# Summing the fetched rows of two of four token tiles in PSUM, in a two-layer decoder kernel

## The chip, the cores and the metric

The kernel runs on one NeuronCore of a Trainium2 chip. The metric is the device time of one execution in microseconds (us); below 0.2% of it, some 3.4 us, a difference cannot be told from none. Engines are named as in the profile: PE is TensorE (PEld its weight loads), ACT is ScalarE, DVE is VectorE, POOL is GpSimd, SP is SyncE with its DMA queue (SPq).

## What is computed

Two layers on 512 tokens of 1024 float32 channels. Layer 0 mixes with a Mamba-2 and sparse-attention pair, layer 1 with a three-branch attention; each layer ends in a hierarchical mixture of experts, and that end is what matters here. Every token goes to two of 32 experts:

```python
for i in range(DEPTH):
    h = rms_norm(x, attn_norm[i])
    x = x + (even_mixer if i % 2 == 0 else odd_mixer)(h, ...)
    h = rms_norm(x, ffn_norm[i])
    x = x + hier_moe(h, ...)

# hier_moe, per token: the weighted sum of its two experts' rows
    def expert_block(args):
        xblk, e = args
        hid = jax.nn.silu(xblk @ w_gate[e]) * (xblk @ w_up[e])
        return hid @ w_down[e]
    yb = lax.map(expert_block, (xb, blk_expert)).reshape(n_rows, dm)
    y = jnp.zeros_like(xt).at[row_token].add(yb * row_weight[:, None].astype(yb.dtype))
```

## The kernel before

Tokens lie in four tiles of 128 (`NT` = 4); the residual `xt` holds them in SBUF, tile `i` as `xt[:, i, :]`. All queues are written by hand in program order, one instruction stream per engine, with semaphores between them.

**Experts.** `per_expert` runs 32 experts over a ring of three weight buffers: the first three, a loop, then experts 30 and 31 by hand (`after` = 1 and 0). For each expert PE multiplies gate and up in two halves (L1807), turns the hidden rows (L1813) and multiplies down (L1820); ACT copies the result out (L1902); POOL scatters 64 x 2 half-rows to `y_d` in DRAM. The last expert's rows are not scattered: behind expert 30, PE turns a matrix of weighted ones (L2078), ACT copies it to `last_T` (L2137), and after expert 31 eight matmuls (L2107) spread its 64 rows over all tokens, two per tile, into banks 2i and 2i+1.

**The end of a layer.** SP fetches the scattered rows back, one DMA per tile with both rows of each token (L2001, semaphores `m_yin0` to `m_yin3`). DVE then adds them tile by tile: `add_fetched(i)` is two instructions over 1024 channels (L2316), `add_last(i)` two over 512 that add PE's banks (L2323) and raise `m_x`. The order is fetched 0, fetched 1, last 0, fetched 2, last 1, fetched 3, last 2, last 3.

**What follows.** In layer 0, `odd_act` takes each tile's squares as it is ready (`norm_square`, L271), POOL makes the reciprocal root (`norm_pool`, L279 and L281), ACT the diagonal (`norm_diag`, L302), PE turns and scales the tile with it (`turn_pe`, L318, 16 recorded instructions a tile), DVE and ACT copy out (L332, L330), and the projection starts when all four are out (L1440). Three matmuls without use (L1431) stand ahead of the turning. In layer 1, SP writes each tile to the output (L2341). A float32 matmul is recorded as two PE instructions. In `moe_pool`, POOL waits at the end of a layer for all four counts of `m_fin`, the semaphore of L2107's tiles, before it goes on to `norm_pool`.

Of the kernel before, what the change touches and what calls it, by code (L numbers as in the profile page):

```python
# [22 lines left out]
P = 128  # L23
# [93 lines left out]
class Chain:  # L117
# [42 lines left out]
    "zeros": ("pads", 1), "y_zero": ("acol_in", 32), "m_fin": ("yd_mm", 4), "m_lturn": ("st_mm", 3), "m_lT": ("sq", 5),  # L160
    "m_lones": ("y_gated", 4), "mx0_yin": ("brow", 2), "mx1_yin": ("relb_ones", 1),
# [37 lines left out]
def build(nc, ins, out):  # L199
    ctx = ExitStack()  # L200
    with ctx:
# [66 lines left out]

        def norm_square(act, i):

            nc.scalar.activation(rows[:, i, :], xt[:, i, :], ACT.Square, scale=DM ** -0.5,  # L271
                                 accum_out=ss[:, i:i + 1]).then_inc(S("norm_sq"), 1)

        def norm_pool(pool, tag):
            for i in range(NT):
                n = NT * WHOLE[tag] + i + 1
# [20 lines left out]
        def norm_diag(act, tag, i):  # L297

            act.wait_ge(S("norm_rstd"), NT * 2 * WHOLE[tag] + i + 1)
            if i >= 2:  # L300
                act.wait_ge(S("turned"), 2 * NT * WHOLE[tag] + 2 * (i - 1))
            nc.scalar.activation(diag[:, i % 2], ident[:], ACT.Copy, scale=rstd[:, i:i + 1]).then_inc(S("diag"), 1)  # L302
# [8 lines left out]
        def turn_pe(pe, tag):  # L311

            for i in range(NT):
                pe.wait_ge(S("diag"), NT * WHOLE[tag] + i + 1)
                for half in range(2):
                    for k in range(4):
                        c = (4 * half + k) * P
                        mm = nc.tensor.matmul(bank[2 * i + half][:, k * P:(k + 1) * P], xt[:, i, c:c + P], diag[:, i % 2],  # L318
                                              start=True, stop=True)
                    mm.then_inc(S("turned"), 1)  # L320

        def turn_evac(eng, tag, i, half, on_act=False):

            eng.wait_ge(S("turned"), 2 * NT * WHOLE[tag] + 2 * i + half + 1)
            d = hT[:, 4 * half:4 * half + 4, i * P:(i + 1) * P]
            b = split(bank[2 * i + half][:, :], 4, P)
# [1071 lines left out]
        def odd_sp(sp):  # L1398
            sp.wait_ge(S("m_x"), 2 * NT)
# [320 lines left out]
        last_n = at(O_LAST + 4 * NT * CAP + NT * P, 3, 2 * NT)  # L1720
        wgu = [at(u * EW, 2, KD, FF) for u in range(RING)]
# [303 lines left out]
        def moe_pe(pe, L):  # L2025
# [33 lines left out]

            def body(e, c, cu, u, after):  # L2060
                gate_up(pe, t, c, cu, u)
# [39 lines left out]
            further(pe, t, L, more, last=lambda n: wait_apart(pe, (S(f"{x}_step"), n * X_STEPS + 1)))  # L2101
            pe.wait_ge(S("m_lT"), past("m_lT") + L + 1)
            pe.wait_ge(S(f"{t}_y"), L * NE + NE + 1)
            for i in range(NT):
                for h in range(2):
                    cs = slice(h * CAP, (h + 1) * CAP)
                    mm = nc.tensor.matmul(bank[2 * i + h][:, :], last_T[cs, i * P:(i + 1) * P], yb[cs, (NE - 1) % RING, :],  # L2107
                                          start=True, stop=True)
                mm.then_inc(S("m_fin"), 1)

        def moe_act(act, L):
# [12 lines left out]
            def body(e, c, cu, u, after):  # L2124
# [25 lines left out]
            further(act, t, L, more)  # L2150

# [21 lines left out]
        def moe_dve(dve, L, link):  # L2173
# [95 lines left out]
            def last_ones(c):  # L2269
# [13 lines left out]
                link(v_.tensor_tensor(flat(other_w[:]), keep, flat(weight[:]), ALU.mult))  # L2283
# [35 lines left out]
            def add_last(i):  # L2319
                dve.wait_ge(S("m_fin"), past("m_fin") + NT * L + i + 1)  # L2320
# [75 lines left out]
```

## Time and profile before

| | us |
|---|---|
| median of 3 runs | 1678.95 (1678.14 to 1682.0) |
| the profiled execution | 1680.21 |
| its span, first to last instruction | 1678.3 |

Mean granted clock of TensorE in the profiled execution: 0.984. Profile rows below give a start, a duration, the engine and line, the operation with what it writes and reads, a count, and in brackets how long the engine stood idle before it and what ended that. Merged rows (x16) run from the first start to the last end.

### The profile page before, as it was taken

What the parts mean: (1) busy time and instruction counts of PE and PEld (TensorE: products, weight loads), DVE (VectorE), ACT (ScalarE), POOL (GpSimd) and SP (SyncE); (2) the same over time, 40 slices, a digit from 0 to 9 for tenths busy, and PEclk for the clock granted to TensorE, in tenths of its full rate; (3) what the DMA queues carried; (4) which work ended last, traced back from release to release, by engine and by line L of the source; (5) the groups of instructions that cost most, each with busy time, mean ns of one, the idle gap of its engine ahead of it and who ended that gap; (6) DMA issues with size and microseconds to landing.
All of it is one profiled execution on the core that took longest, in us unless ns stands there. A gap on an engine that the chain in (4) does not pass through costs nothing.

```text
span 1678.3 us, 21100 instructions
## 1 busy us (share of the span) xinstructions
PE 1592.5 (95%) x7988; PEld 754.8 (45%) x7988; DVE 449.7 (27%) x1146; ACT 395.2 (24%) x899; POOL 199.4 (12%) x296
## 2 busy tenths in 40 slices
PE   7999899799999999999899989999799999999995
PEld 4545574433333333333446447865333333333332
DVE  1585751520000000001412235653500000000004
ACT  2444451211111111111200236642211111111110
POOL 2241220000000000000101012330000000000000
PEclk9999999899999999999999999999899999999999
DMA  7620217369999999999914120033699999999997
GB/s 238 260 92 7 101 17 301 138 260 420 422 421 421 421 422 422 422 422 402 347 16 176 60 67 1 1 153 149 251 387 422 421 422 422 422 422 422 421 422 315
DMA packets 118057, 475.25 MB, mean 283 GB/s; under 512 B 40309, under 2 KB 46709, under 8 KB 68076
## 3 DMA queue, kind: packets, MB, share of 16 engines
q1 hardware_dynamic: 109900, 458.02, 68.1%
q10 hardware_dynamic: 3136, 8.40, 1.3%
q0 software_dynamic: 4960, 8.04, 1.3%
q8 instruction: 36, 0.59, 0.2%
q14 instruction: 25, 0.20, 0.0%
HBM read 455.88 MB, written 26.77 MB: 288 GB/s over the span
## 4 chain that ended last, share of the span: by engine, by line
PE 77%; SPq 11%; DMA 4%; DVE 4%; issue 2%; ACT 1%; POOL 1%; DVEq 0%; ACTq 0%; POOLq 0%
PE bank L1807 19%; PE bank L1820 9%; SPq L1755 9%; PE bank L1782 8%; PE bank L1440 8%; PE bank L560 7%; PE bank L813 6%; PE bank L448 4%; DMA arena<-in_moe_w_up 3%; PE bank L413 3%; PE bank L1797 2%; PE bank L430 2%; PE bank L894 2%; SPq L1764 1%; PE bank L1813 1%
## 5 line engine op out<-in xcount | busy, mean ns | idle before, releaser
L1807 PE MATMUL bank<-arena 128*64 128x512 f32 x2048 | 451.4, 592 | 7.4 <-DMA arena<-in_moe_w_up 6.1
L1807 PEld LDWEIGHTS bank<-arena 128*64 128x64 f32 x2048 | 143.6, 137 | 302.7 <-issue 291.0
L1820 PE MATMUL bank<-arena 128*64 128x512 f32 x1024 | 230.6, 592 | 2.1 <-DVE arena L1911 2.1
L1907 DVE TENSOR_TENSOR arena<-arena,bank 128x256 f32<-128x256 f32 x64 | 26.9, 420 | 638.5 <-ACT arena L1897 638.5
L1782 PE MATMUL bank<-arena 128*64 128x512 bf16 x1280 | 167.4, 393 | 9.7 <-DVE arena L1777 6.4
L1826 POOL DMA_INDIRECT y_d<-arena,slot_row x62 | 60.7, 979 | 874.3 <-ACT arena L1902 874.3
L1440 PE MATMUL bank<-arena 128*128 128x512 f32 x320 | 138.1, 593 | 0.8 <-ACT arena L330 0.8
L1820 PEld LDWEIGHTS bank<-arena 128*64 128x64 f32 x1024 | 71.9, 137 | 124.1 <-issue 110.5
L1897 ACT ACTIVATE arena<-bank 128x256 f32<-128x256 f32 x64 | 24.5, 383 | 407.6 <-PE bank L1807 407.6
L560 PE MATMUL bank<-arena 128*128 128x512 f32 x256 | 113.6, 601 | 0.0
L813 PE MATMUL bank<-arena 128*128 128x512 f32 (+1 forms) x288 | 105.3, 525 | 0.0
L1782 PEld LDWEIGHTS bank<-arena 128*64 128x64 bf16 x1280 | 69.4, 113 | 68.7 <-issue 10.5
L1440 PEld LDWEIGHTS bank<-arena 128*128 128x128 f32 x320 | 60.6, 190 | 77.1 <-issue 76.1
L448 PE MATMUL bank<-arena 128*128 128x128 f32 (+1 forms) x544 | 83.1, 278 | 3.8 <-DVE arena L478 2.9
L1902 ACT ACTIVATE arena<-bank 128x512 f32<-128x512 f32 x64 | 38.2, 597 | 190.1 <-PE bank L1820 190.1
L1793 ACT ACTIVATE gain<-bank 128x512 f32<-128x512 f32 x64 | 38.2, 597 | 179.0 <-PE bank L1782 179.0
L448 PEld LDWEIGHTS bank<-arena 128*128 128x128 f32 x544 | 70.8, 191 | 12.5 <-DVE arena L478 5.9
L560 PEld LDWEIGHTS bank<-arena 128*128 128x128 f32 x256 | 48.5, 192 | 57.5 <-issue 57.5
L813 PEld LDWEIGHTS bank<-arena 128*128 128x128 f32 x288 | 49.8, 190 | 54.5 <-issue 54.5
L504 DVE CUSTOM_DVE_ANT_0 arena<-bank,arena 128x512 f32<-128x512 f32 (+3 forms) x128 | 52.4, 415 | 65.6 <-PE bank L413 45.5
L413 PE MATMUL bank<-arena 128*128 128x31 f32 (+8 forms) x256 | 68.2, 405 | 1.6 <-ACT arena L1565 0.9
L1911 DVE COPY arena<-bank 128x256 f32<-128x256 f32 x64 | 27.2, 424 | 132.0 <-PE bank L1813 132.0
(302 smaller groups left out, 1458.8 us busy)
## 6 DMA issues: line engine op xcount, KB each, us to landing
arena<-in_moe_w_gate SPq DMA_DIRECT2D x128, 1024.0 KB, 20.0
arena<-in_moe_w_up SPq DMA_DIRECT2D x128, 1024.0 KB, 22.8
arena<-in_moe_w_down SPq DMA_DIRECT2D x62, 2048.0 KB, 23.2
arena<-in_even_w_in SPq DMA_DIRECT2D x4, 2048.0 KB, 8.1
y_d<-arena ACTq DMA_DIRECT2D x2, 4096.0 KB, 16.8
arena<-y_d SPq DMA_DIRECT2D x8, 1024.0 KB, 9.1
arena<-bias_row_d SPq DMA_DIRECT2D x2, 3584.0 KB, 11.6
arena<-in_odd_w_in SPq DMA_DIRECT2D x3, 2048.0 KB, 7.8
```

What stands on the lines that cost most here:

```text
L413: mm = nc.tensor.matmul(score_bank[u["a"] % 4][:, 0:u["L"]], u["q"], u["k"], start=True, stop="mask" not in u)
L448: mm = nc.tensor.matmul(bank[4 + u["m"] % 2][:, u["b"] * D:(u["b"] + 1) * D], self.pT[0:w, u["a"] % 2, kt, :], u["v"](kt), start=(kt == 0) ...
L504: ins_ = nc.vector.tensor_tensor_reduce(out=self.p[:, u["a"] % 4, 0:L], in0=score_bank[u["a"] % 4][:, 0:L], in1=u["bias"], scale=-1.0, sca ...
L560: mm = nc.tensor.matmul(mix_bank(n)[:, :], mixT[:, k, i * P:(i + 1) * P], wo[half][:, k, :], start=(k == 0), stop=(k == KD - 1))
L813: mm = nc.tensor.matmul(o, l, r, start=(k == 0), stop=(k == KD - 1))
L1440: mm = nc.tensor.matmul(o, lhs(k), rhs(k), start=(k == 0), stop=(k == KD - 1))
L1755: sp.dma_start(wgu[u][:, n, 4 * h:4 * h + 4].rearrange("p (e j) f -> p e (j f)", e=1), src).then_inc(S(f"{t}_{('wgu', 'wgv')[h]}{u}"), 16)
L1782: mm = nc.tensor.matmul(bank[4][h * CAP:(h + 1) * CAP, :], pick[:, i, :], parts[part][i][:, h * 512:(h + 1) * 512], start=(part == 0 and i ...
L1793: return nc.scalar.activation(xe, bank[4][:, :], ACT.Copy)
L1807: mm = nc.tensor.matmul(bank[1][fh * CAP:(fh + 1) * CAP, :], xeT[:, j, half * CAP:(half + 1) * CAP], wgu[u][:, :, n, fh * FH:(fh + 1) * FH ...
L1820: mm = nc.tensor.matmul(bank[3][dh * CAP:(dh + 1) * CAP, :], hidT[:, j, fh * CAP:(fh + 1) * CAP], wd[u][:, n, dh * 512:(dh + 1) * 512], st ...
L1826: return nc.gpsimd.indirect_dma_start(out=y_d[layer][:, :], out_offset=bass.IndirectOffsetOnAxis(ap=slot_row[:, n:n + 1], axis=0), in_=yb[ ...
```

## The change

For tiles 0 and 1, PE adds everything in PSUM (banks 4 to 7): the residual through the identity, the two fetched rows of each token through diagonals of their weights, and the last expert. Then they are copied out: tile 0 by ACT, tile 1 by DVE (in layer 1, one half by ACT). DVE still adds tiles 2 and 3. The tiles are finished, normed and turned in the order 0, 2, 3, 1 (`FIN`); the squares of a tile now stand ahead of the diagonal of the tile before on ACT; the three matmuls at L1431 are gone. In the first layer's entry only the banks differ. A branch that runs when an expert has over 64 rows is changed too; it is not taken in the profile before.

```diff
+        FIN = (0, 2, 3, 1)
+        TILE_SEQ = {"n0": tuple(range(NT)), "n2": FIN}
+        def fin_bank(i, h):
+            return bank[(4 + 2 * i + h) % 8]
...
         def odd_sp(sp):
-            sp.wait_ge(S("m_x"), 2 * NT)
+            for i in range(NT):
+                summed(sp, 0, i)
...
         def odd_pe(pe):
-            pe.wait_ge(S("m_x"), 2)
-            for _ in range(3):
-                nc.tensor.matmul(bank[0][:, :], ident[:], wd[1][:, 0, 0:512], start=True, stop=True)
             turn_pe(pe, "n2")
...
-            for i in range(NT):
-                act.wait_ge(S("m_x"), 2 * i + 2)
+            for n, i in enumerate(FIN):
+                summed(act, 0, i)
                 norm_square(act, i)
-                norm_diag(act, "n2", i)
+                if n:
+                    norm_diag(act, "n2", n - 1)
+            norm_diag(act, "n2", NT - 1)
...
+            def residuals(start=True, stop=False):
+                for i in range(2):
+                    for h in range(2):
+                        nc.tensor.matmul(fin_bank(i, h)[:, :], ident[:], xt[:, i, h * 512:(h + 1) * 512], start=start, stop=stop)
+            def fetched_rows(i):
+                pe.wait_ge(S("m_wdiag"), past("m_wdiag") + 4 * L + 2 * i + 2)
+                pe.wait_ge(S(f"{t}_yin{i}"), 16 * (L + 1))
+                for h in range(2):
+                    for k in range(2):
+                        nc.tensor.matmul(fin_bank(i, h)[:, :], w_diag[:, i, k], y_rows[:, k, i, h * 512:(h + 1) * 512],
+                                         start=False, stop=False)
+            def last_rows(i):
+                for h in range(2):
+                    cs = slice(h * CAP, (h + 1) * CAP)
+                    mm = nc.tensor.matmul(fin_bank(i, h)[:, :], last_T[cs, i * P:(i + 1) * P], yb[cs, (NE - 1) % RING, :],
+                                          start=(i >= 2), stop=True)
+                mm.then_inc(S("m_fin"), 1)
             def body(e, c, cu, u, after):
+                if after == 0:
+                    pe.wait_ge(S("m_lT"), past("m_lT") + L + 1)
+                    residuals()
                 gate_up(pe, t, c, cu, u)
...
-            for i in range(NT):
-                for h in range(2):
-                    cs = slice(h * CAP, (h + 1) * CAP)
-                    mm = nc.tensor.matmul(bank[2 * i + h][:, :], last_T[cs, i * P:(i + 1) * P], yb[cs, (NE - 1) % RING, :],
-                                          start=True, stop=True)
-                mm.then_inc(S("m_fin"), 1)
+            fetched_rows(0)
             pe.wait_ge(S(f"{t}_y"), L * NE + NE + 1)
+            last_rows(0)
+            last_rows(2)
+            last_rows(3)
+            fetched_rows(1)
+            last_rows(1)
...
                     nc.scalar.activation(last_T, bank[7][:, :], ACT.Copy).then_inc(S("m_lT"), 1)
+                    act.wait_ge(S("m_other"), past("m_other") + L + 1)
+                    for i in range(2):
+                        for k in range(2):
+                            nc.scalar.activation(w_diag[:, i, k], ident[:], ACT.Copy,
+                                                 scale=other_w[:, k, i:i + 1]).then_inc(S("m_wdiag"), 1)
...
+            for n, i, halves in ((0, 0, (0, 1)), (NT - 1, 1, (0,) if L else ())):
+                if halves:
+                    act.wait_ge(S("m_fin"), past("m_fin") + NT * L + n + 1)
+                for h in halves:
+                    nc.scalar.activation(xt[:, i, h * 512:(h + 1) * 512], fin_bank(i, h)[:, :], ACT.Copy).then_inc(S("m_xa"), 1)
...
-            add_fetched(0)
-            for i in range(1, NT):
-                add_fetched(i)
-                add_last(i - 1)
-            add_last(NT - 1)
+            dve.wait_ge(S("m_other"), past("m_other") + L + 1)
+            add_fetched(2)
+            add_fetched(3)
+            add_last(2)
+            add_last(3)
+            dve.wait_ge(S("m_fin"), past("m_fin") + NT * (L + 1))
+            for h in range(2) if L == 0 else (1,):
+                v_.tensor_copy(xt[:, 1, h * 512:(h + 1) * 512], fin_bank(1, h)[:, :]).then_inc(S(f"{t}_x"), 1)
...
-            for i in range(NT):
-                sp.wait_ge(S("m_x"), 2 * NT + 2 * i + 2)
+            for i in FIN:
+                summed(sp, 1, i)
                 sp.dma_start(out[0, i * P:(i + 1) * P, :], xt[:, i, :]).then_inc(S("out"), 16)
```

PE of the kernel before, at the end of layer 0's experts, from the last expert's down product (L1820) to the first turned tile (L318); waits in brackets are semaphores (`m_y` is the last expert's copied rows, `sq` stands for `m_lT`):

```order
L1820 MATMUL bank<-arena 64x512 x7
...
L2107 MATMUL bank<-arena 128x512 [waits m_y,sq]
L2107 MATMUL bank<-arena 128x512 x7
L1431 MATMUL bank<-arena,ident 128x512 [waits m_x]
L1431 MATMUL bank<-arena,ident 128x512 x2
L318 MATMUL bank<-gain,arena 128x128 [waits diag]
```

PE of the changed kernel at the same place; L2090 is `fetched_rows`, L2097 `last_rows`, L334 the turning, and `ix_relu` stands for `m_wdiag`:

```order
L2090 MATMUL bank<-arena 128x512 [waits m_yin0,ix_relu]
L2090 MATMUL bank<-arena 128x512 x3
L2097 MATMUL bank<-arena 128x512 [waits m_y]
L2097 MATMUL bank<-arena 128x512 x5
L2090 MATMUL bank<-arena 128x512 [waits m_yin1,ix_relu]
L2090 MATMUL bank<-arena 128x512 x3
L2097 MATMUL bank<-arena 128x512 x2
L334 MATMUL bank<-gain,arena 128x128 [waits diag]
```

Eight matmuls of the fetched rows now stand around those of the last expert, and the last count of `m_fin` is raised behind all of them. PE of the changed kernel ahead of expert 31, where L2122 turns the weighted ones and L1825 is gate and up:

```order
L2122 MATMUL bank<-ident,arena 128x128 [waits y_gated]
L2122 MATMUL bank<-ident,arena 128x128 x3
L2082 MATMUL bank<-arena,ident 128x512 [waits sq]
L2082 MATMUL bank<-arena,ident 128x512 x3
L1825 MATMUL bank<-arena 64x512 [waits m_wgu1,m_hid,m_xT]
L1825 MATMUL bank<-arena 64x512 x7
L1825 MATMUL bank<-arena 64x512 [waits m_wgv1]
```

Four residual matmuls (L2082) stand between the two, behind a wait for ACT's copy. POOL's stream is the same in both; in the changed kernel the first norm operations behind the experts of layer 0 read (`yd_mm` stands for `m_fin`):

```order
L294 TENSOR_SCALAR ss<-ss 128x1 [waits yd_mm,norm_sq]
L296 TENSOR_TENSOR rstd<-ss,nhalf 128x1 [waits norm_ms]
L294 TENSOR_SCALAR ss<-ss 128x1 [waits norm_sq]
L296 TENSOR_TENSOR rstd<-ss,nhalf 128x1 [waits norm_ms]
L294 TENSOR_SCALAR ss<-ss 128x1 [waits norm_sq]
```

The first of them carries the wait for `m_fin`, whose value is reached with the tile that now comes last.

## Rows read from the trace of the kernel before

**Rows 1.** The page: span, busy time of PE, the chain by engine.

```profile
PE 1592.5 (95%) x7988; PEld 754.8 (45%) x7988; DVE 449.7 (27%) x1146; ACT 395.2 (24%) x899; POOL 199.4 (12%) x296
PE 77%; SPq 11%; DMA 4%; DVE 4%; issue 2%; ACT 1%; POOL 1%; DVEq 0%; ACTq 0%; POOLq 0%
```

**Rows 2.** The chain of waits in order of time, end of layer 0: start, us, what.

```profile
814.91 1.30 DVE arena L2323 x2
...
818.68 1.14 ACT arena L271 x2
...
824.14 76.20 PE bank L1440 x177
```

**Rows 3.** Timeline of PE, end of layer 0: start, us, work, idle before.

```profile
787.83 0.66 PE L2078 MATMUL bank<-ident,arena 128*128 128x128 f32 x4
789.22 3.65 PE L1807 MATMUL bank<-arena 128*64 128x512 f32 x16 [0.72 <-DMA arena<-in_moe_w_up]
794.26 3.65 PE L1807 MATMUL bank<-arena 128*64 128x512 f32 x16 [1.39 <-DMA arena<-in_moe_w_up]
...
799.93 3.65 PE L1820 MATMUL bank<-arena 128*64 128x512 f32 x16 [0.52 <-DVE arena L1911]
804.37 3.70 PE L2107 MATMUL bank<-arena 64*128 64x512 f32 x16 [0.79 <-ACT arena L1902]
...
815.79 2.05 PE L318 MATMUL bank<-gain,arena 128*128 128x128 f32 x16 [1.79 <-ACT gain L302]
...
821.26 2.05 PE L318 MATMUL bank<-gain,arena 128*128 128x128 f32 x16 [0.38 <-ACT gain L302]
```

**Rows 4.** Timeline of DVE, end of layer 0.

```profile
801.93 5.25 DVE L2316 SCALAR_TENSOR_TENSOR arena<-arena,other_w 128x1024 f32<-128x1024 f32 x4 [2.06 <-DMA arena<-y_d]
...
814.91 2.48 DVE L2323 TENSOR_TENSOR arena<-arena,bank 128x512 f32<-128x512 f32 x4
```

**Rows 5.** Timeline of ACT, end of layer 0.

```profile
788.53 0.60 ACT L2137 ACTIVATE arena<-bank 128x512 f32<-128x512 f32 x1
...
803.63 0.60 ACT L1902 ACTIVATE arena<-bank 128x512 f32<-128x512 f32 x1 [5.29 <-PE bank L1820]
...
818.37 0.40 ACT L302 ACTIVATE gain<-ident,rstd 128x128 f32<-128x128 f32 x1 [0.99 <-POOL rstd L281]
...
822.46 1.14 ACT L330 ACTIVATE arena<-bank,acol 128x128 f32<-128x128 f32 x4 [1.25 <-PE bank L318]
```

**Rows 6.** Timeline of POOL, end of layer 0.

```profile
810.08 1.39 POOL L281 TENSOR_TENSOR rstd<-ss,nhalf 128x1 f32<-128x1 f32 x1
...
817.47 0.22 POOL L279 TENSOR_SCALAR ss<-ss 128x1 f32<-128x1 f32 x1 [2.17 <-ACT arena L271]
817.77 0.57 POOL L281 TENSOR_TENSOR rstd<-ss,nhalf 128x1 f32<-128x1 f32 x1
```

**Rows 7.** Line 2001, the four fetches, layer 0 and then layer 1.

```profile
L2001 SPq DMA_DIRECT2D arena<-y_d x4: 606/613/692, 795.9 to 797.9; - x4
...
DMA to landing us min/median/max: 6.0/9.3/12.5
...
L2001 SPq DMA_DIRECT2D arena<-y_d x4: 599/614/726, 1654.3 to 1656.2; - x4
...
DMA to landing us min/median/max: 5.4/8.8/12.2
```

**Rows 8.** Timeline and waits, end of layer 1: PE, DVE, SP, SP's last wait.

```profile
1661.95 3.70 PE L2107 MATMUL bank<-arena 64*128 64x512 f32 x16 [0.79 <-ACT arena L1902]
1672.67 2.48 DVE L2323 TENSOR_TENSOR arena<-arena,bank 128x512 f32<-128x512 f32 x4
1673.98 1.53 SPq L2341 DMA_DIRECT2D out_x<-arena  x2
SPq L201 <- DMA out_x<-arena: 2.4, 1, 2.4
```

**Rows 9.** Stretches: length, busy time by engine, granted clock, DMA share, GB/s.

```profile
816.00:820.00 4.00, 3.02 (x26) 2.83 (x26) 3.78 (x7) 2.59 (x5) 0.89 (x3) 1.00 1.09 350
...
1670.00:1672.00 2.00, 0.00 (x0) 0.00 (x0) 1.96 (x3) 0.00 (x0) 0.00 (x0) 0.56 0.52 211
```

More of the change, by code:

```diff
@@ L274, in norm_pool @@
         def norm_pool(pool, tag):
-            for i in range(NT):
-                n = NT * WHOLE[tag] + i + 1
+            for n, i in enumerate(TILE_SEQ[tag], NT * WHOLE[tag] + 1):
                 pool.wait_ge(S("norm_sq"), n)
@@ L295, in mix_pool, with norm_diag @@
                 nc.gpsimd.tensor_tensor(rstd[:, i:i + 1], s_, nhalf[:, 0:1], ALU.pow).then_inc(S("norm_rstd"), 1)
[L297 to L302, printed above, removed]
+        def norm_diag(act, tag, n):
+            act.wait_ge(S("norm_rstd"), NT * 2 * WHOLE[tag] + n + 1)
+            if n >= 2:
+                act.wait_ge(S("turned"), 2 * NT * WHOLE[tag] + 2 * (n - 1))
+            i = TILE_SEQ[tag][n]
+            nc.scalar.activation(diag[:, n % 2], ident[:], ACT.Copy, scale=rstd[:, i:i + 1]).then_inc(S("diag"), 1)
         def norm_row(dve, tag, i):
@@ L311, in turn_pe @@
         def turn_pe(pe, tag):
-            for i in range(NT):
-                pe.wait_ge(S("diag"), NT * WHOLE[tag] + i + 1)
+            for n, i in enumerate(TILE_SEQ[tag]):
+                pe.wait_ge(S("diag"), NT * WHOLE[tag] + n + 1)
                 for half in range(2):
@@ L317, in turn_pe, with turn_evac @@
                         c = (4 * half + k) * P
-                        mm = nc.tensor.matmul(bank[2 * i + half][:, k * P:(k + 1) * P], xt[:, i, c:c + P], diag[:, i % 2],
+                        mm = nc.tensor.matmul(fin_bank(i, half)[:, k * P:(k + 1) * P], xt[:, i, c:c + P], diag[:, n % 2],
                                               start=True, stop=True)
                     mm.then_inc(S("turned"), 1)
-        def turn_evac(eng, tag, i, half, on_act=False):
-            eng.wait_ge(S("turned"), 2 * NT * WHOLE[tag] + 2 * i + half + 1)
+        def turn_evac(eng, tag, n, half, on_act=False):
+            eng.wait_ge(S("turned"), 2 * NT * WHOLE[tag] + 2 * n + half + 1)
+            i = TILE_SEQ[tag][n]
             d = hT[:, 4 * half:4 * half + 4, i * P:(i + 1) * P]
-            b = split(bank[2 * i + half][:, :], 4, P)
+            b = split(fin_bank(i, half)[:, :], 4, P)
             g = acol[:, WHOLE[tag], 4 * half:4 * half + 4]
@@ L2100, in more, with begin_anew @@
                 down_mms(0).then_inc(S(f"{x}_step"), 1)
-            further(pe, t, L, more, last=lambda n: wait_apart(pe, (S(f"{x}_step"), n * X_STEPS + 1)))
-            pe.wait_ge(S("m_lT"), past("m_lT") + L + 1)
-            pe.wait_ge(S(f"{t}_y"), L * NE + NE + 1)
-            for i in range(NT):
-                for h in range(2):
-                    cs = slice(h * CAP, (h + 1) * CAP)
-                    mm = nc.tensor.matmul(bank[2 * i + h][:, :], last_T[cs, i * P:(i + 1) * P], yb[cs, (NE - 1) % RING, :],
-                                          start=True, stop=True)
-                mm.then_inc(S("m_fin"), 1)
+            def begin_anew(n):
+                wait_apart(pe, (S(f"{x}_step"), n * X_STEPS + 1))
+                residuals()
+                pe.wait_ge(S(f"{x}_yin"), past(f"{x}_yin") + 16 * NT)
+            further(pe, t, L, more, first=lambda: residuals(start=False, stop=True), last=begin_anew)
+            fetched_rows(0)
+            pe.wait_ge(S(f"{t}_y"), L * NE + NE + 1)
+            last_rows(0)
[3 more added lines that the diff above has]
+            last_rows(1)
         def moe_act(act, L):
```

16 lines of the change are left out of this document (12 added, 4 removed).

## The prediction

> **What bounds the kernel now.** I read the page first: PE is busy 95% of the span and makes up 77% of the chain [rows 1]. The change touches two short places, the ends of the two layers, so the chain there matters more than shares. At the end of layer 0 it runs on DVE's adds, whose last pair ends at 816.21 for tile 2 [rows 2], then over POOL and ACT to the squares of tile 3 at 818.68 and to the projection (L1440) at 824.14, from where PE works for 76.20 us without a gap [rows 2]. DVE starts at 801.93, when the first fetch lands, and ends all adds at 814.91 + 2.48 = 817.39 [rows 4]. PE is done with its eight matmuls at 804.37 + 3.70 = 808.07 [rows 3] and then waits for the others: 1.79 us ahead of the second turned tile [rows 3]. In layer 1 the same adds end at 1672.67 + 2.48 = 1675.15, and SP's last wait, for the output, follows [rows 8]. So DVE is late by 9.3 us against PE (817.39 to 808.07), and that is what the change goes at.
>
> **The price of PE's new work.** A full float32 matmul is two records. 177 records took 76.20 us [rows 2], 0.43 us each, so 0.86 us a matmul. The records of gate, up and down and of L2107 run in pairs, 16 in 3.65 to 3.70 us with a tail of some 0.22 [rows 3]: 0.215 us each, and 0.86 us for one tile of L2107. Per layer PE gets 4 residual matmuls (3.44 us) and 8 for fetched rows (6.88 us); DVE loses four of eight adds of 5.25 / 4 = 1.31 us [rows 4].
>
> **Residuals, ahead of expert 31.** They wait for ACT's copy of bank 7, which ends at 788.53 + 0.60 = 789.13 [rows 5]; with 0.14 us to wake PE (804.37 [rows 3] less the end of a 0.60 us copy that began at 803.63 [rows 5]) they start at 789.27 and end at 792.71. The first half of gate and up moves from 789.22 there. The second half came at 794.26 after 1.39 us of waiting for weights [rows 3], so 1.39 us and a little more are hidden: now it follows at 792.71 + 3.44 = 796.15 and ends at 799.80 instead of 797.91. Silu, hidden rows and down all move by **1.89 us**. No transfer waits for it: the fetch is issued from 795.9 [rows 7] behind expert 30.
>
> **Behind expert 31.** Down starts at 799.93 + 1.89 = 801.82 and lets the next matmul in at 805.26. The first four fetched matmuls need tile 0's rows, landed at 801.93 [rows 4], and run to 808.70, over the 0.8 us that PE had waited for ACT's copy [rows 3]. Then 0.86 us each for last rows of tiles 0, 2 and 3 (811.28), 3.44 us for the fetched rows of tile 1 (814.72) and 0.86 us for its last rows: 815.58, with the tail **815.8**. PE's end thus moves from 808.07 by 7.7 us: 1.89 + 6.88, less 0.8 and rounding.
>
> DVE: the four fetches are issued from 795.9 to 797.9 and take 6.0, 9.3 in the middle and 12.5 us [rows 7], so tile 3's rows land at 810.4. Its two adds end at 813.0, the four of L2323's kind at 815.5 (2.48 us [rows 4]), and the copies of tile 1 follow PE, 815.85 to 817.1. So tile 1 is whole at 817.1, as late as the last tile before (817.39). The four diagonals of weights on ACT cost at most 0.40 us each [rows 5] and lie in its idle time before silu: nothing.
>
> **The wait that stays.** POOL's first norm operation waits for all four counts of `m_fin`. Before, these were there at 808.07, ahead of any tile's squares. Now the last comes at 815.8, though tile 0 is copied out by about 811 and could be normed. Behind that wait stand all of POOL's norm work, ACT's diagonals and PE's turning. First root: 815.85 + 0.22 + 0.57 and gaps of 0.08 = 816.7 [rows 6]; the diagonal 0.40 more [rows 5]; turning starts at 817.16. A tile's 16 records take 2.05 us with the tail, 1.89 in a row [rows 3], so four take until 824.88, and every later diagonal (I get about 818.6, 820.0 and 821.5) is ready in time. The copy-out before took 824.14 - 823.31 = 0.83 us [rows 2, 3]. The projection starts at **825.7**, against 824.14: **+1.57 us**, and the freed order of squares on ACT gives nothing back, since PE's turning is what is late.
>
> POOL's root is 1.39 us in one row and 0.57 in another [rows 6]; the long one lies beside DVE's adds of two SBUF operands, the short one beside copies out of PSUM. From the new 815.85 on DVE only copies from PSUM, so I take 0.57; with 1.39 for the first alone the start is 0.82 later, the upper bound of this term. On this the Trainium skill ("SBUF — State Buffer", "SBUF: two separate sides") says that VectorE and GpSimd share a port pair as an exclusive lock, also when a VectorE operation has two SBUF inputs; the two rows agree, and by it the 1.39 would not appear here at all.
>
> From L1440 on, PE has no gap for a long while, so the delay goes through to the end; the lower bound is that a later wait swallows it (0). SP's third chunk of weights for the projection, which waits for the last `m_fin` too, comes 7.7 us later; it is needed only behind the two chunks before it, 27.5 us each (32 matmuls x 0.86), and has that cover: nothing.
>
> **Layer 1.** The same sequence, 1661.95 - 804.37 = 857.58 us later [rows 3, 8]: PE ends at 1673.4. DVE has tile 3's rows at 1656.2 + 12.2 = 1668.4 [rows 7], ends its adds at 1668.4 + 2.62 + 2.48 = 1673.5 and its half copy of tile 1 at 1674.25; ACT's half (0.60 [rows 5]) ends at 1674.0. Before, the last add ended at 1675.15 [rows 8]: -0.9 us. The last two output tiles are now issued about 0.7 us apart and not 1.2, and may queue for 0.5 of it, so -0.4 to -0.9; I take **-0.65 us**.
>
> **Sum.** +1.57 - 0.65 = **+0.9 us**. Against the profiled execution, 1680.21, that is 1681.1; against the median of the runs shown, 1.26 lower, it is **1679.9 us**. It is well inside the 0.2% (3.4 us) that a measurement of this kernel can tell from no change.
>
> **Rivals.** (a) *The roots and diagonals pace the turning.* If every root takes 1.39 us, POOL needs 1.39 + 0.30 a tile, the fourth root is ready at 815.85 + 6.8 = 822.6, the projection starts at about 826.1 or, with ACT's waits for turned tiles between, 827: total +1.3 to +2.2, 1680.3 to 1681.2. For it: the two long roots of the trace; against it: what DVE does by then. (b) *PE's extra work is off the path* and only DVE's end counts, tile 1 whole at 816.8 and 5.46 us (818.68 to 824.14 [rows 2]) from its squares to the projection: 822.3, -1.8, with layer 1's -0.65 in all -2.5: 1676.5. Against it: the start of the turning and four tiles in a row on PE; it would need POOL not to wait. (c) *Slower: the clock falls.* The three matmuls ahead of the turning are gone, and PE now stands idle between 815.8 and 817.16 in one piece. At 1670 to 1672 the granted clock was 0.56, PE having been idle since 1665.65; at 816 to 820, after an idle of 1.79 us, it was 1.00 [rows 3, 8, 9]. [...] The Trainium skill ("TensorE: Matmul & The Clock Gate", Part 1) holds that the throttled state is the default and activity releases it, which speaks for matmuls without use in such a gap; the trace agrees for the long idle and not for the short. (d) *It gains over 3.4 us.* If the full matmuls of the sums cost what the packed ones do (0.43 us and not 0.86), PE saves 5.2 us per layer of the above: the turning starts at 812 and waits for tiles 2 and 3 alone, which end at 815.5; then the projection starts at some 821.5, -2.6, and with layer 1's -0.9 it is 1675.4. Every row with 128 contracted rows and 128 columns speaks against it.
>
> **How the numbers follow.** Forecast 0.56; (a) 0.2; (b) 0.15; (c) 0.05; (d) 0.04. Forecast, (a) and (b) are all within 0.2% of the time before. The three runs shown lie between 0.8 below and 3.1 above their median, so I move 0.03 to either side for a median that falls off: faster 0.07, same 0.85, slower 0.08. The range goes down to (b), 1676.5, which also takes in the forecast's own low end (the delay swallowed, -0.9, and the runs' -0.8: 1677.2); it goes up to the forecast's high end (+1.57 + 0.82 - 0.4 = +2.0, 1681.0) and (a), with half of the runs' upward scatter: 1682.5. Left out are (c), (d) and the outer scatter.
>
> **What would show it.** Residuals (L2082) at 789.3 and the second gate half ending at 799.8; the last PE matmul of the sums at 815.8 and 1673.4; POOL's first norm operation of layer 0 held until then, not by the squares, with ACT's first diagonal waiting for it; the turning in one piece of 7.5 us; L1440 at 825.7; the last DVE copy ending at 1674.25. Wrong would be: diagonals that PE waits for between the tiles (a), L1440 before 824 (b), a granted clock below 1 between 816 and 826 (c), or a last output issue later than 1675.2.

## The result, and the profile after

The changed kernel takes 1685.74 us (median of 20 runs, 1683.05 to 1690.44), the kernel before 1681.85 us beside it on the same chip (median of 20, 1678.14 to 1685.26). The ratio is 1.0024, 95% interval 1.0017 to 1.0031: **+4.0 us**, between 2.9 and 5.2. That is slower: the ratio is just beyond the 0.2% line, though its interval begins below that, and the time is outside the forecast's range.

The page of the changed kernel (answers to [rows 1]; span, busy time of the engines, the chain by engine):

```profile
span 1683.0 us, 21185 instructions
PE 1610.6 (96%) x8028; PEld 762.9 (45%) x8030; DVE 437.2 (26%) x1133; ACT 400.0 (24%) x912; POOL 197.7 (12%) x296
PE 80%; SPq 10%; DMA 4%; DVE 3%; ACT 2%; issue 1%; POOL 0%; DVEq 0%; ACTq 0%; POOLq 0%
```

The shares say only that DVE lost some work to PE. To find 4 us in 1683, cut the span at rows that both traces have. `ones` is PE's turning of the weighted ones behind expert 30, `proj` the first projection matmul, `gate` the first full block of gate and up in layer 1, `down` its first down. All numbers are differences of starts in PE's timeline, in us, the last column to the end of the span:

| kernel | ones to proj | proj to gate | gate to down | down to ones | ones to end |
|---|---|---|---|---|---|
| before | 36.31 | 371.28 | 19.20 | 430.79 | 32.89 |
| after | 38.62 | 371.21 | 20.41 | 430.78 | 34.32 |
| before, second profile | 36.31 | 373.24 | 20.55 | 430.57 | 32.82 |
| before, third | 36.32 | 373.29 | 19.37 | 430.89 | 32.83 |
| after, second | 38.62 | 372.63 | 20.56 | 430.49 | 34.24 |
| after, third | 38.61 | 373.23 | 20.47 | 430.72 | 34.25 |

The first and the last column repeat to 0.1 us. They are the two places that the change touches, and they hold +2.31 and +1.43 us, +3.7 together, against +4.0 timed. The second and third column wander by 1 to 2 us in both kernels. The stretch ahead of the first column wanders more: `ones` starts at 787.83, 787.81 and 790.70 us in the three profiles of before and at 787.66, 791.46 and 790.82 us in those of after. That alone is as large as the change, so the total of one profile can't be used for it.

PE at the end of layer 0, after (answers to [rows 3]):

```profile
789.00 3.70 PE L2082 MATMUL bank<-arena,ident 128*128 128x512 f32 x8 [0.69 <-ACT arena L2185]
792.63 7.09 PE L1825 MATMUL bank<-arena 128*64 128x512 f32 x32
...
801.68 3.65 PE L1838 MATMUL bank<-arena 128*64 128x512 f32 x16 [0.52 <-DVE arena L1929]
805.26 3.70 PE L2090 MATMUL bank<-arena 128*128 128x512 f32 x8
808.89 2.85 PE L2097 MATMUL bank<-arena 64*128 64x512 f32 x12
811.67 3.70 PE L2090 MATMUL bank<-arena 128*128 128x512 f32 x8
815.30 1.13 PE L2097 MATMUL bank<-arena 64*128 64x512 f32 x4
818.03 7.41 PE L334 MATMUL bank<-gain,arena 128*128 128x128 f32 x64 [1.60 <-ACT gain L318]
826.28 9.25 PE L1455 MATMUL bank<-arena 128*128 128x512 f32 x21 [0.83 <-ACT arena L347]
```

L2082 are the residuals, L2090 the fetched rows, L2097 the last expert, L334 the turning, L1455 the projection. PE sums without a gap from 801.68 to 816.43, stands for 1.60 us, and turns all four tiles in one piece. What it waits for in those 1.60 us stands in POOL's, ACT's and DVE's timelines (answers to [rows 6], [rows 5] and [rows 4]):

```profile
816.66 0.23 POOL L294 TENSOR_SCALAR ss<-ss 128x1 f32<-128x1 f32 x1 [26.55 <-PE bank L2097]
816.97 0.58 POOL L296 TENSOR_TENSOR rstd<-ss,nhalf 128x1 f32<-128x1 f32 x1
```

```profile
811.19 1.06 ACT L287 ACTIVATE arena<-arena 128x1024 f32<-128x1024 f32 x1
812.15 0.19 ACT L287 ACTIVATION_READ_ACCUMULATOR arena<-arena 128x1 f32 x1
...
817.58 0.40 ACT L318 ACTIVATE gain<-ident,rstd 128x128 f32<-128x128 f32 x1 [2.27 <-POOL rstd L296]
```

```profile
806.97 2.61 DVE L2374 SCALAR_TENSOR_TENSOR arena<-arena,other_w 128x1024 f32<-128x1024 f32 x2 [5.35 <-DMA arena<-y_d]
810.20 2.61 DVE L2374 SCALAR_TENSOR_TENSOR arena<-arena,other_w 128x1024 f32<-128x1024 f32 x2 [0.62 <-DMA arena<-y_d]
812.84 2.48 DVE L2381 TENSOR_TENSOR arena<-arena,bank 128x512 f32<-128x512 f32 x4
816.48 1.29 DVE L2389 COPY arena<-bank 128x512 f32<-128x512 f32 x2 [1.16 <-PE bank L2097]
```

Tile 0 has its squares at 812.34, and POOL leaves them until PE's last L2097 is over: it starts at 816.66, 4.3 us later. DVE's adds end at 815.32 instead of 817.39 [rows 4], and nobody gains from it.

The end of layer 1, after (answers to [rows 8]): PE and DVE in the timeline, then the instructions of the block's closing line, with duration in ns and start. A DRAIN is an engine's last step, in which it lets its own work run out:

```profile
1676.33 1.13 PE L2097 MATMUL bank<-arena 64*128 64x512 f32 x4
1677.50 0.69 DVE L2389 COPY arena<-bank 128x512 f32<-128x512 f32 x1 [0.93 <-PE bank L2097]
```

```profile
L202 POOLq DRAIN  x1: 5141/5141/5141, 1677.6 to 1677.6; - x1
L202 SPq COMPARE_BRANCH  x1: 38/38/38, 1680.8 to 1680.8; - x1
```

SP has seen its last output land by 1680.8; the program still can't end, since POOL's drain takes 5.14 us from 1677.6 and ends at 1682.8. The same line of the kernel before:

```profile
L201 POOLq DRAIN  x1: 5141/5141/5141, 1665.8 to 1665.8; - x1
...
L201 SPq COMPARE_BRANCH  x1: 38/38/38, 1677.9 to 1677.9; - x1
```

There the drain ended at 1670.9, seven microseconds ahead of the output.

### The profile page after: what moved, and what is told of

Its sections match the earlier page's. It is cut to its first block, busy times and chain, and to the rows that moved or that the text cites. A ratio compares the mean times of both kernels' runs of the same rounds, so it can differ in the third digit from the quotient of the medians.

```text
span 1683.0 us, 21185 instructions
## 1 busy us (share of the span) xinstructions
PE 1610.6 (96%) x8028; PEld 762.9 (45%) x8030; DVE 437.2 (26%) x1133; ACT 400.0 (24%) x912; POOL 197.7 (12%) x296
## 4 chain that ended last, share of the span: by engine, by line
PE 80%; SPq 10%; DMA 4%; DVE 3%; ACT 2%; issue 1%; POOL 0%; DVEq 0%; ACTq 0%; POOLq 0%
PE bank L1825 20%; PE bank L1838 10%; SPq L1773 9%; PE bank L1800 8%; PE bank L1455 8%; PE bank L577 7%; PE bank L830 6%; PE bank L465 4%; DMA arena<-in_moe_w_up 3%; PE bank L430 3%; PE bank L1815 2%; PE bank L911 2%; PE bank L447 2%; SPq L1782 1%; PE bank L1831 1%
## 5 line engine op out<-in xcount | busy, mean ns | idle before, releaser
L1825 PE MATMUL bank<-arena 128*64 128x512 f32 x2048 | 451.0, 593 | 3.1 <-DMA arena<-in_moe_w_up 1.7
L1825 PEld LDWEIGHTS bank<-arena 128*64 128x64 f32 x2048 | 143.4, 137 | 299.1 <-issue 292.1
L1455 PE MATMUL bank<-arena 128*128 128x512 f32 x320 | 138.1, 593 | 0.8 <-ACT arena L347 0.8
L1455 PEld LDWEIGHTS bank<-arena 128*128 128x128 f32 x320 | 60.7, 190 | 77.0 <-issue 76.0
```

What stands on the lines that cost most here:

```text
L1455: mm = nc.tensor.matmul(o, lhs(k), rhs(k), start=(k == 0), stop=(k == KD - 1))
L1825: mm = nc.tensor.matmul(bank[1][fh * CAP:(fh + 1) * CAP, :], xeT[:, j, half * CAP:(half + 1) * CAP], wgu[u][:, :, n, fh * FH:(fh + 1) * FH ...
```

## The experiments

All ratios are to the kernel before, run beside it on the same chip: one chip for the first four kernels below, one for the repeats of both kernels, one for the last four.

### No wait of POOL at the end of layer 1

```diff
-            pool.wait_ge(S("m_fin"), past("m_fin") + NT * (L + 1))
-            pool.sem_inc(S(f"{t}_yfree"), 1)
+            if L == 0:
+                pool.wait_ge(S("m_fin"), past("m_fin") + NT * (L + 1))
+                pool.sem_inc(S(f"{t}_yfree"), 1)
```

> The changed kernel, but POOL no longer waits for m_fin at the end of layer 1 (it still does in layer 0). Theory P (POOL's drain of 5.14 us, which starts after that wait at 1677.6 and ends at 1682.8, sets the end of the changed kernel): span shorter by 1.7 to 1.9 us than the changed kernel's, and from the last copy of tile 1 to the span's end about 3.1 us as before the change and not 4.8; start of the projection unchanged at +2.1 us against before. Rival D (the output writes, now issued closer together, are what ends late): no change of the end, 4.8 us stay. Against the kernel before: P +2.2 us, D +4.

Measured: 1685.56 us, ratio 1.0020 (1.0010 to 1.0030). Ones to end is 32.53 us instead of 34.32. The closing line of this kernel:

```profile
L202 POOLq DRAIN  x1: 5141/5141/5141, 1657.1 to 1657.1; - x1
...
L202 SPq COMPARE_BRANCH  x1: 38/38/38, 1680.1 to 1680.1; - x1
```

The drain is as long as before but starts 20 us earlier, and the span now ends right behind the output: 3.02 us after DVE's last copy (1677.48 to 1680.5), where after has 4.81 (1678.19 to 1683.0). Before, these two ends lay 3.15 us apart (1675.15 to 1678.3), so the last two outputs, issued close together, cost nothing. POOL's wait and its drain are worth 1.8 us in the trace, more than the whole +1.43 us of layer 1. The times alone could not show it: the ratios 1.0024 and 1.0020 have overlapping intervals.

### No wait of POOL in layer 0 either

The wait goes in both layers; `m_yfree` is raised after the norm instead. The squares' throwaway results go to other tiles' space, since POOL's wait had also kept them off rows that PE still reads.

```diff
-            nc.scalar.activation(rows[:, i, :], xt[:, i, :], ACT.Square, scale=DM ** -0.5,
+            nc.scalar.activation(rows[:, i % 3, :], xt[:, i, :], ACT.Square, scale=DM ** -0.5,
...
+            pool.wait_ge(S("m_fin"), past("m_fin") + NT)
+            pool.sem_inc(S("m_yfree"), 1)
...
-            pool.wait_ge(S("m_fin"), past("m_fin") + NT * (L + 1))
-            pool.sem_inc(S(f"{t}_yfree"), 1)
```

> As the run before, and in layer 0 the wait for m_fin stands behind POOL's four norm operations; the unused squares of tile 3 are written to another place so that they don't fall on rows that PE still reads. Theory W (POOL's wait holds back the turning): the first diagonal is ready at about 815.6, the turning starts when PE is done with the sums, 816.4 and not 818.03, and L1440's work starts at 824.7 and not 826.3: 1.6 us less than the run before, +0.6 us against the kernel before. Rival Q (PE's own queue is the bound and the wait is hidden by it): under 0.3 us less. Rival F (the 1.2 us that the changed kernel's profile loses at the start of layer 1's experts is caused by the change): it stays in every run.

Measured: 1682.39 us, ratio 0.9998 (0.9988 to 1.0009). Ones to proj falls from 38.62 to 36.94 us. PE's timeline, and ACT's first diagonal:

```profile
818.72 1.13 PE L2099 MATMUL bank<-arena 64*128 64x512 f32 x4
819.78 7.41 PE L334 MATMUL bank<-gain,arena 128*128 128x128 f32 x64
```

```profile
818.49 0.39 ACT L318 ACTIVATE gain<-ident,rstd 128x128 f32<-128x128 f32 x1
```

The brackets are gone: the turning follows the sums at once, because the first diagonal is ready at 818.88, ahead of the end of the sums. The wait was worth 1.68 us. PE still needs 0.6 us more than before (36.94 against 36.31), now with no wait between the sums and the turning.

### Without the residual matmuls

Tiles 0 and 1 are summed without their residual, which this kernel leaves out of the result; everything else stands.

```diff
-                                          start=False, stop=False)
+                                          start=(k == 0), stop=False)
...
-                    residuals()
```

> The changed kernel without the four residual matmuls per layer; the residual is left out of tiles 0 and 1 in both layers, so that part of the computation is missing, and the data that follow differ. Theory R (they cost what the gap between the halves of gate and up does not hide): the last PE matmul of the sums comes 1.9 to 2.1 us earlier in both layers, the projection too; total 3.8 to 4.2 us less than the changed kernel, so within 0.5 us of the kernel before. Rival H (they are hidden, the fetched rows are the whole price): under 1 us less.

Measured: 1679.07 us, ratio 0.9988 (0.9978 to 0.9998). Ones to proj is 36.65 us, 1.97 less than after, for 3.44 us of PE work taken out: the forecast's 1.89 for what they cost on the path was right, the rest lay in the wait for weights. Ones to end falls by 1.55, for the same reason. The two ends together stand 0.2 us above those of before, yet the time is 2.0 us below (0.3 to 3.7), and 6 below after where 3.8 to 4.2 was expected. In the profile, 0.9 us is missing between down and ones, and 1.25 us ahead of the first `ones` (786.58 against 787.83), a stretch that wanders by more than this in the unchanged kernels. The values after layer 0 are others here, so the total of this run proves little; the two ends do.

### The residual in pieces

The same sums, with the four residual matmuls spread: one ahead of the gate halves, one between them, one behind, one behind the turned hidden rows.

```diff
+                    residual(0, 0)
+                    gate_up(pe, t, c, cu, u, between=lambda: residual(0, 1))
+                    residual(1, 0)
...
-                    residuals()
-                gate_up(pe, t, c, cu, u)
+                else:
+                    gate_up(pe, t, c, cu, u)
...
+                if after == 0:
+                    residual(1, 1)
```

> The changed kernel with its four residual matmuls per layer spread: one ahead of expert 31's gate, one between the halves of gate and up, one behind them, one behind the turned hidden rows, where PE stood idle 0.69, 1.39, 0.94 and 0.52 us. Theory R: they cost 0.2 to 0.8 us per layer and not 1.9, so 1.1 to 1.7 us less per layer, 2.2 to 3.4 in all against the changed kernel. Rival S (each switch between full and packed matmuls costs about 0.2 us of its own): six more switches take 1.2 us of that back, gain under 0.7 us per layer.

Measured: 1682.68 us, ratio 1.0009 (0.9997 to 1.0020). Both ends are shorter than in after: 36.97 instead of 38.62, and 32.65 instead of 34.32. PE's timeline:

```profile
787.36 1.02 PE L2081 MATMUL bank<-arena,ident 128*128 128x512 f32 x2
788.31 3.65 PE L1825 MATMUL bank<-arena 128*64 128x512 f32 x16
791.89 1.13 PE L2081 MATMUL bank<-arena,ident 128*128 128x512 f32 x2
793.29 3.65 PE L1825 MATMUL bank<-arena 128*64 128x512 f32 x16 [0.27 <-DMA arena<-in_moe_w_up]
796.87 1.13 PE L2081 MATMUL bank<-arena,ident 128*128 128x512 f32 x2
797.97 0.47 PE L1831 MATMUL bank<-ident,arena 128*128 128x128 f32 x2
```

The second gate half starts where the weights let it, 6.43 us behind the ones (786.86), as before (794.26 - 787.83 [rows 3]). One residual fills the wait for weights, and one the wait for DVE's hidden rows (1.00 us ahead of L1813 in before); a block of four in front of everything could not. The gain of 1.65 and 1.67 us is what theory R said; rival S wanted under 0.7. POOL's wait is still in this kernel, and its drain (from 1675.0) still closes the span, though by little, since SP is past its last output at 1679.9; it comes earlier only because PE does.

### Is the rest chance? Both kernels again, twice

The first pair of profiles differs by 1.2 us between gate and down of layer 1, where the change does nothing. The granted clock falls there in both; the windows of after and then of before (length, busy time of PE, PEld, DVE, ACT, POOL, granted clock, DMA share, GB/s):

```profile
1212.00:1214.00 2.00, 1.83 (x10) 0.86 (x12) 0.44 (x2) 0.00 (x0) 0.00 (x0) 0.50 0.99 412
1214.00:1216.00 2.00, 2.00 (x11) 0.70 (x8) 0.00 (x0) 0.00 (x0) 0.00 (x0) 0.50 0.58 227
1216.00:1218.00 2.00, 2.00 (x12) 0.86 (x13) 0.42 (x1) 0.00 (x0) 0.00 (x0) 0.57 0.02 8
```

```profile
1210.00:1212.00 2.00, 1.90 (x10) 0.89 (x12) 0.38 (x2) 0.00 (x0) 0.00 (x0) 0.50 0.95 338
1212.00:1214.00 2.00, 2.00 (x16) 0.85 (x12) 0.17 (x1) 0.00 (x0) 0.00 (x0) 0.79 0.16 64
1214.00:1216.00 2.00, 2.00 (x16) 0.85 (x14) 0.68 (x2) 0.60 (x1) 0.00 (x0) 1.00 0.00 0
```

In both kernels PE has stood idle for 2.56 us just before, and starts again at 1212.17 in after, 1210.10 in before. A mean of 0.79 in the second window of before puts the return to 2.4 GHz at 1212.8; 0.57 in the last window of after puts it at 1217.7. So PE works 2.7 us at 1.2 GHz in before and 5.5 us in after (in the first two windows behind the wait 26 records start in before and 21 in after). Is that the change, or chance? Both kernels ran unchanged twice more.

> The kernel before, unchanged, profiled once more. The stretch from layer 1's first gate to its first down product took 19.20 us in its first profile and 20.4 in all four two-tile kernels that kept the residual. Theory C (chance: where the clock's fall lies against PE's wait of 2.56 us): it takes other values than 19.2 in some profile of this kernel, between 17.9 and 20.5, while the stretches at the layers' ends (36.3 and 32.9 us) repeat within 0.1. Rival F (it belongs to the changed kernel): 19.2 again here.

> The kernel before, a third profile; as for the second: theory C lets the stretch be anything from 17.9 to 20.5 us, rival F wants 19.2.

> The changed kernel, unchanged, profiled once more. Theory C: the stretches at the layers' ends repeat (38.6 and 34.3 us), that at the start of layer 1's experts need not be 20.4 again. Rival F: 20.4 again.

> The changed kernel, a third profile; theory C lets the stretch be anything from 17.9 to 20.5 us, rival F wants 20.4.

Measured, one time each: before 1683.26 and 1685.38 us, after 1689.93 and 1689.90 us, before beside them once more 1679.59. These single times lie further apart than 4.0 us; between the second profiles, 6.7 us apart in span, 3.7 are the two ends and 3.65 lie ahead of the first `ones`. The table above has the stretches: the second profile of before shows 20.55 us, as long as after, the third 19.37. The kernel before in that long case (windows of 3 us; PE starts at 1212.04 there):

```profile
1212.00:1215.00 3.00, 2.96 (x14) 1.24 (x16) 0.31 (x1) 0.00 (x0) 0.00 (x0) 0.50 0.74 257
1215.00:1218.00 3.00, 3.00 (x16) 1.17 (x14) 0.42 (x1) 0.00 (x0) 0.00 (x0) 0.52 0.01 3
```

So the 1.2 us can come without the change. After showed the long case in all three of its profiles, and so did the variants without POOL's wait and with the residual in pieces (20.40, 20.46, 20.41 us); before showed it in one of three. The variant without the residual took 19.14 us, and the kernel with one tile, below, 19.37. That is too few to rule out that the two-tile kernels meet the long case more often.

### Matmuls without use in the waits of the router

To see what the clock's fall is worth, five matmuls without use go ahead of the counting of experts and three ahead of the first hidden rows, in both layers, where PE stands for 5.3 and 2.6 us. Once on top of after, once on top of before; the code added is the same:

```diff
+        def filler(n):
+            for _ in range(n):
+                nc.tensor.matmul(bank[7][:, :], ident[:], xt[:, 0, 0:512], start=True, stop=True)
...
+            filler(5)
...
+                if isinstance(c, int) and c == L * NE:
+                    filler(3)
```

> The changed kernel with matmuls of no use into a free bank (bank 7), five 128x512 float32 ones where PE waits for the router's one-hots (idle 5.26 us in both traces) and three where it waits for the picks of the third expert (2.56 us), in both layers. Theory C (the 1.2 us that the changed kernel's profile loses between its first gate and its first down product of layer 1, 20.4 us against 19.2, is the granted clock standing at half for 6.6 us instead of 3.2, by where its fall happens to lie): with the gaps filled the clock stays up, that stretch is the same in this run and its partner on the kernel before, 18 to 19 us, and the two differ by 3.7 us alone, the 2.3 of layer 0's end and the 1.4 of layer 1's. Rival F (the change lengthens the routing of layer 1): the stretch stays over 1 us longer here than in the partner.

> The kernel before with the same matmuls without use. Theory C: first gate to first down of layer 1 takes 18 to 19 us and not 19.2, no granted clock at half between 1180 and 1220, and the whole is 2 to 5 us shorter than the kernel before, since the picks ahead of the first expert also ran at half clock (1182 to 1192). Rival N (these matmuls delay what they stand in front of as much as the clock gives back): within 1 us of the kernel before.

Measured: on top of before 1678.33 us, ratio 0.9984 (0.9970 to 0.9998); on top of after 1687.13 us, 1.0029 (1.0019 to 1.0039). Gate to down is 17.85 us in both, against 19.1 to 20.6 without: the fall of the clock was the price of this stretch. On before, `ones` of layer 0 starts at 784.93 instead of 787.83; this may be a gain as well, but the start wanders by 3 us in the unchanged kernel, and the one-tile kernel below has it at 785.97 without the fill. The clock did not stay up everywhere: it was at 0.50 from 1187 to 1190 in this kernel, which I had excluded. And the two kernels came out 7.6 us apart by the ratios (4.9 above before and 2.7 below), not the 3.7 expected. The reason shows in the timeline of PE and one window, filled after:

```profile
799.90 3.65 PE L1838 MATMUL bank<-arena 128*64 128x512 f32 x16 [0.52 <-DVE arena L1929]
805.79 5.40 PE L2095 MATMUL bank<-arena 128*128 128x512 f32 x8 [2.24 <-issue]
```

```profile
807.00:808.00 1.00, 1.00 (x2) 0.34 (x2) 0.96 (x2) 0.00 (x0) 0.00 (x0) 0.50 1.07 395
```

PE waits 2.24 us ahead of the fetched rows, for nothing that the profile shows: the first fetch was issued at 793.9 and landed 6.0 us later. PE then works for a microsecond at 2.4 GHz (mean 0.92 from 806 to 807) and on at 1.2: eight records in 5.40 us instead of 3.70. Ones to proj becomes 42.64 us, 4.0 more than after. In layer 1 the same place has 0.89 us of it. In none of the other profiles does such a gap appear at these two places, and nothing near it was edited; the matmuls added earlier move what follows in PE's program. One rival fits and was not tested: PE takes a branch at 801.0, past the code for experts with over 64 rows, and one packet of instructions is moved inside the gap (803.2 to 805.8); in after the branch is at 802.6 and the packet comes only behind 805.2, beside the eight matmuls. Whether PE stood for its instructions no run shows, and the cause stays open.

### One tile instead of two

Everything learnt, in one kernel: only tile 2 is summed in PSUM (two residual matmuls, one ahead of the gate halves and one between them, and four for fetched rows), PE takes the last rows of tiles 0, 1 and 3 first, the order is 0, 1, 2, 3, and POOL does not wait.

```diff
-        FIN = (0, 2, 3, 1)
+        FIN = (0, 1, 2, 3)
...
-            fetched_rows(0)
...
+            for i in (0, 1, 3):
+                last_rows(i)
+            fetched_rows(2)
...
-            last_rows(3)
-            fetched_rows(1)
-            last_rows(1)
```

> A version made from the findings: PE sums one tile only, tile 2, whose rows land third (the last expert's rows of tiles 0, 1 and 3 come first); its two residual matmuls stand in the two waits of expert 31 (0.69 and 1.39 us); DVE adds tiles 0, 1 and 3; POOL does not wait for m_fin ahead of its norms or at the end. From the row ends: DVE starts at the first landing as before and ends 1.31 x 6 + 0.62 x 6 and a short wait for tile 3 later, about 3.2 us before the kernel before; PE is done 2.4 us ahead of that. Theory: the stretch from the turned ones of expert 30 to the projection takes 32 to 33 us (before 36.3, changed 38.6), that from the ones of layer 1 to the span's end 29.7 to 30.5 (before 32.9, changed 34.3); in all 6 to 7 us less than the kernel before. Rival (the turning on PE is the bound wherever the tiles come from): layer 0 gains under 2 us.

Measured: 1678.14 us, ratio 0.9973 (0.9961 to 0.9984): **faster than before**. Ones to proj 34.17 us, ones to end 30.37, so -2.14 and -2.52 against before, -4.7 together and -4.5 timed. PE at the end of layer 0:

```profile
806.29 3.67 PE L2100 MATMUL bank<-arena 128*128 128x512 f32 x8 [0.99 <-DMA arena<-y_d]
809.89 1.13 PE L2107 MATMUL bank<-arena 64*128 64x512 f32 x4
810.95 2.05 PE L337 MATMUL bank<-gain,arena 128*128 128x128 f32 x16
813.68 5.62 PE L337 MATMUL bank<-gain,arena 128*128 128x128 f32 x48 [0.68 <-ACT gain L321]
820.14 15.26 PE L1458 MATMUL bank<-arena 128*128 128x512 f32 x35 [0.83 <-ACT arena L350]
```

The turning begins 25 us behind the ones (810.95 - 785.97), against 30.4 in after, and loses 0.68 us to the second diagonal, which stands behind ACT's copy and squares of tile 2. Its root is a long one too, beside DVE's adds (DVE and POOL):

```profile
808.75 2.61 DVE L2378 SCALAR_TENSOR_TENSOR arena<-arena,other_w 128x1024 f32<-128x1024 f32 x2 [0.82 <-DMA arena<-y_d]
810.20 1.58 POOL L299 TENSOR_TENSOR rstd<-ss,nhalf 128x1 f32<-128x1 f32 x1
```

I had expected 32 to 33 us for the stretch and got 34.17, and 6 to 7 us in all and got 4.5; only layer 1 came out as said (29.7 to 30.5). The rival, that the turning on PE is the bound of layer 0 wherever the tiles come from, has the mechanism right: the turning follows the sums without a wait. Its figure, under 2 us, was missed by 0.14.

### One tile, with the filled waits

```diff
+            filler(5)
...
+                if isinstance(c, int) and c == L * NE:
+                    filler(3)
```

> The version before with the matmuls without use of the first two runs. If both effects are apart they add: 6 to 7 us from the one tile and what the partner on the kernel before shows for the filled gaps. If the sum is smaller by over 1 us, one takes what the other gives.

Measured: 1673.49 us, ratio 0.9944 (0.9929 to 0.9958), the fastest of all. It is 9.2 to 9.4 us below before. The one tile (-4.5) and the fill (-2.7) give 7.2 apart; the 2 us above that lie within their intervals. Here PE has no gap of issue, and ones to proj is 33.64 us.

## Why the prediction was wrong

The forecast was 1679.9 us, the time is 1685.74. Of those 5.8 us half is the base: I set +0.9 on the median of three runs, 1678.95, and twenty runs of the same kernel gave 1681.85, 2.9 higher. The other half, 2.9 us, is the change: +0.95 forecast, +3.9 by the medians. Three terms were off; the two inside the change add up to 2.1 us in layer 1 and 0.7 in layer 0.

**The step that failed: layer 1.** I forecast -0.4 to -0.9 from the end of DVE's last copy and let SP's last wait set the end. In layer 0 the prediction follows POOL's wait for `m_fin`; in layer 1, where the same wait stands, it does not mention it, since no norm is behind it. But POOL's closing drain is behind it, 5.14 us long, and it was in the trace of before, hidden by 7 us. It sets the end now: +1.8 us, and without the wait they go (the first experiment). The cost of queueing between the last two outputs, which I did allow for, was nothing. So layer 1 came to +1.43 us instead of -0.65: from the last copy to the end it is 4.81 us, where 3.15 and 0.25 for the queue were forecast, and the last copy itself is 0.67 us later, by the next term.

**The term mis-sized: PE's sums.** They end 28.77 us behind `ones` in layer 0 (816.43 - 787.66) where 27.97 was forecast (815.8 - 787.83), and 28.78 in layer 1 where 27.99 was forecast (1673.4 - 1645.41). The counts and the prices in a row were right, but a group costs more where the next is of the other kind, full (128 rows and 128 columns) or packed (64 of either). Eight full records take 3.63 us until the next group starts (805.26 to 808.89) and not 3.44, twelve packed ones 2.78 (808.89 to 811.67) and not 2.58, the sixteen of down 3.58 (801.68 to 805.26) and not 3.44. The three full groups make 0.57 us of it, the packed ones 0.34, the last tail 0.05, and the waits for ACT and DVE were 0.16 shorter than forecast: +0.8 us in each layer. What in the change of kind costs this, no run separates. The trace of before had it already; behind this row the next group starts at 787.83 [rows 3], 3.58 us later:

```profile
784.25 3.65 PE L1820 MATMUL bank<-arena 128*64 128x512 f32 x16 [0.56 <-DVE arena L1911]
```

The prediction's "less 0.8 and rounding" hides it too: 1.89 + 6.88 - 0.8 is 8.0 and not 7.7. With this term layer 0 came to +2.31 instead of +1.57, and tile 1 of layer 1 was whole 0.23 us earlier than before (29.51 against 29.74 behind `ones`), not 0.9.

**The base.** See above; the range went up by half the three runs' scatter, and the true median lay beyond that.

**What held.** The path through the rest of layer 0 was right. From the end of the sums to the projection I forecast 9.9 us, and 9.85 passed (816.43 to 826.28); that it fits so closely is luck, since the first diagonal took 1.60 us and not 1.36, and the turning 7.41 and not 7.72. POOL's first operation was held by PE's last matmul, not by the squares; the roots took 0.58 and 0.57 us and not 1.39, the first of them (from 816.97) wholly beside DVE's copies out of PSUM (816.48 to 817.77); the turning was one piece; the residuals cost 1.97 us on the path where 1.89 was said. The Trainium skill ("SBUF — State Buffer", "SBUF: two separate sides") had it that two SBUF inputs of a VectorE operation lock GpSimd out, and the trace agrees in that the long root did not come back once DVE had none. In the one-tile kernel, where DVE has two again, it did: 1.58 us. Waiting and residuals are each undone by an experiment (-1.68, -1.65), and with both remedies and one tile less the kernel gains 4.5 us.

**The rivals.** (a) is out: no diagonal was waited for between the tiles. (b) is out as the kernel stands, since POOL did wait; with the wait gone PE's own work still set the pace (36.94 against 36.31 us), so it was half wrong in itself. (c) did not happen in layer 0: the granted clock was 1.00 from 814 to 826, through an idle of 1.60 us. Filled after shows what it would have looked like: a gap of 2.24 us, and a microsecond behind it 0.50. (d) is out: the full matmuls cost what their records said, and a little more. None of my rivals was the one that decided, a wait that holds up an engine's closing step.

## What to carry to other kernels

When a change makes an engine wait longer, follow that engine to its last instruction, its drain included, in every place where the code runs; a wait that guards nothing in the last layer still delays the end. Spread fill-in matmuls over the waits that exist (for weights, for another engine's result) instead of putting them in one block ahead of them, and move only as much work to the busiest engine as fits in its idle time. One tile gained 4.5 us where two lost 4.0, but not by the smaller share alone: the one-tile kernel also has the residuals spread and POOL's wait gone. Two tiles with both remedies were not run. An estimate from the rows puts them some 2 us below before: layer 0 at 38.62 - 1.68 - 1.65 = 35.3 us against 36.31, layer 1 at 28.7 (the last copy behind `ones` with the residuals in pieces, 1676.48 - 1647.75) + 3.02 = 31.8 against 32.89. So about half of the gain would be left for the smaller share; that is argued and not shown. Three runs do not give a median to 0.1%; where the forecast change is smaller than their scatter, widen the range by all of it.

## What was unexpected in the hardware

- POOL's drain at the end of the program takes 5.14 us in every trace of this case, whenever it starts; DVE's took 0.73 us and ACT's 0.63 at the same place in after, and DVE's 2.51 in before, where its last adds still ran.
- A group of float32 matmuls ahead of one of the other kind costs 0.14 to 0.20 us more than its records in a row: 3.63 against 3.44 us for eight full ones, 2.78 against 2.58 for twelve packed ones, 3.58 against 3.44 for sixteen.
- After the same idle of 2.56 us, PE worked 2.7 us at the lower clock in one execution and nearly 6 in another of the same kernel (1212.04 until about 1217.9); gate to down was 19.20 and 20.55 us.
- PE stood 2.24 us ahead of a matmul whose rows had landed, in a kernel whose only edit lies elsewhere in its program. The cause is open.
